# Sums of squares split before and after the product's end, and root and reciprocal on a 128x2 column of tokens, for the norms behind w_o and w_down

## The reference, cut to what matters

```python
def rms_norm(x, g):
    xf = x.astype(jnp.float32)
    y = xf * lax.rsqrt(jnp.mean(xf * xf, axis=-1, keepdims=True) + NORM_EPS)
    return (y * g.astype(jnp.float32)).astype(x.dtype)
...
        m = jnp.concatenate([a, p], axis=-1) @ w_o[l]
        x = x + rms_norm(m, post_mix_g[l])
        h = rms_norm(x, pre_ffn_g[l])
        up = causal_dwconv(h @ w_up[l], conv_w[l], conv_b[l])
        y = (jax.nn.gelu(up[..., :D_FF], approximate=True) * up[..., D_FF:]) @ w_down[l]
        x = x + rms_norm(y, post_ffn_g[l])
    return x
```

## Time and profile before

| | |
|---|---|
| time, median of 3 runs | 2281.69 us (2281.61 to 2284.61) |
| profiled execution: its time | 2283.57 us |
| profiled execution: its span on the core | 2281.8 us |
| PE busy | 2164.8 us (95%), 15448 instructions |
| DVE busy | 1486.6 us (65%) |
| ACT busy | 1077.4 us (47%) |
| POOL busy | 83.1 us (4%) |

### The profile page before, as it was taken

How to read it: one execution, slowest core, us unless ns; L and a number is a source line. 1 busy time by engine, 2 the same in 40 slices (tenths; PEclk the granted TensorE clock), 3 DMA queues, 4 the chain that set the end, 5 groups by cost and what they waited for, 6 DMA issues and landing times.

```text
span 2281.8 us, 39887 instructions
## 1 busy us (share of the span) xinstructions
PE 2164.8 (95%) x15448; PEld 1854.4 (81%) x15448; DVE 1486.6 (65%) x2015; ACT 1077.4 (47%) x1502; POOL 83.1 (4%) x70
## 2 busy tenths in 40 slices
PE   7999989999999999999899999987798999999996
PEld 6888868888888888887687878877686888888885
DVE  6656558885588856875974588853475544566654
ACT  5444555444444434445544655433343543556533
POOL 0800000000000000000000000002110000000000
PEclk9999989999999999999899999999999999999998
DMA  8654545665566556655355455643353555644551
GB/s 274 205 162 156 166 130 180 188 188 189 185 191 185 188 189 187 191 165 185 130 202 167 157 161 165 210 122 74 99 176 125 175 184 193 185 142 145 167 192 57
DMA packets 402679, 384.04 MB, mean 168 GB/s; under 512 B 43441, under 2 KB 401073, under 8 KB 401713
## 3 DMA queue, kind: packets, MB, share of 16 engines
q1 hardware_dynamic: 402546, 382.18, 53.9%
HBM read 374.78 MB, written 7.34 MB: 167 GB/s over the span
## 4 chain that ended last, share of the span: by engine, by line
PE 86%; DVE 8%; issue 2%; ACT 2%; DMA 1%; SPq 0%; DVEq 0%; POOL 0%; ACTq 0%
PE acc L746 44%; PE acc L749 22%; PE acc L770 3%; PE aux L1035 2%; PE acc L825 2%; PE acc L826 2%; PE acc L827 2%; PE acc L773 2%; DVE w_lo L1862 2%; PE acc L1035 1%; PE aux L843 1%; ACT w_hi L1274 1%; PE aux L1196 1%; PE aux L950 1%; PE aux L970 1%
## 5 line engine op out<-in xcount | busy, mean ns | idle before, releaser
L1862 DVE TENSOR_TENSOR w_lo<-raw_w,w_hi 128x1024 fp32r<-128x1024 f32 (+1 forms) x592 | 714.9, 1228 | 471.6 <-ACT w_hi L1274 470.5
L1274 ACT ACTIVATE w_hi<-raw_w 128x1024 fp32r<-128x1024 f32 (+1 forms) x592 | 613.0, 1046 | 686.3 <-PE acc L749 575.0
L746 PE MATMUL acc<-h,w_hi 128*128 128x512 f32 x1664 | 525.9, 397 | 1.2 <-DVE w_lo L1862 1.2
L749 PEld LDWEIGHTS acc<-h,w_lo 128*128 128x128 f32 x1664 | 312.6, 188 | 73.8
L749 PE MATMUL acc<-h,w_lo 128*128 128x256 f32 x1664 | 327.1, 278 | 0.0
L746 PEld LDWEIGHTS acc<-h,w_hi 128*128 128x128 f32 x1664 | 254.5, 189 | 2.2 <-issue 1.4
L746 PE MATMUL acc<-x_split,w_hi 128*128 128x512 f32 x704 | 225.2, 401 | 0.0
L746 PE MATMUL acc<-ff,w_hi 128*128 128x512 f32 x704 | 221.6, 396 | 2.4 <-DVE ff L2107 2.4
L746 PE MATMUL acc<-xs_b,w_hi 128*128 128x512 f32 x512 | 162.5, 399 | 1.7 <-DVE w_lo L2300 0.9
L749 PEld LDWEIGHTS acc<-ff,w_lo 128*128 128x128 f32 x704 | 132.2, 188 | 31.3
L749 PEld LDWEIGHTS acc<-x_split,w_lo 128*128 128x128 f32 x704 | 132.2, 188 | 31.2
(11 more groups left out here) (333 smaller groups left out, 3124.9 us busy)
## 6 DMA issues: line engine op xcount, KB each, us to landing
raw_w<-in_w_up SPq DMA_DIRECT2D x176, 512.0 KB, 3.5
raw_w<-in_a_w_in SPq DMA_DIRECT2D x128, 512.0 KB, 3.7
raw_w<-in_w_in SPq DMA_DIRECT2D x64, 512.0 KB, 4.0
raw_w<-in_w_down SPq DMA_DIRECT2D x64, 512.0 KB, 3.5
raw_w<-in_b_w_qg SPq DMA_DIRECT2D x64, 512.0 KB, 3.8
raw_w<-in_w_o SPq DMA_DIRECT2D x32, 512.0 KB, 3.5
raw_w<-in_a_w_out SPq DMA_DIRECT2D x32, 512.0 KB, 3.6
raw_w<-in_w_k_shared SPq DMA_DIRECT2D x32, 512.0 KB, 3.6
```

What stands on the lines that cost most here:

```text
L746: pe.matmul(ACC[2 * b + f], WHI[:, q, k, f * P:(f + 1) * P], op[:, kt, :, :].rearrange("p h t -> p (h t)"), start=first, stop=False)
L749: mm = pe.matmul(ACC[2 * b + f][:, 0:T], WLO[:, slot, k, f * P:(f + 1) * P], op[:, kt, 0, :], start=False, stop=last)
L1274: act.activation(WHI[:, u % 4, 0:ku, :], RAWW[:, u, 0:ku, :], ACT.Copy).then_inc(hi_made, 1)
L1862: dve.tensor_tensor(WLO[:, u, 0:ku, :], RAWW[:, u, 0:ku, :], WHI[:, u % 4, 0:ku, :].bitcast(F32), ALU.subtract)\
```

## The change

PE: the product and its sums become one function, `scaled_norm_gemm`. The sums of tiles 8 to 11 follow unit 27 instead of unit 31, and the last four tiles are no longer summed by `four_sums`. After the product `token_sums` takes the strips of the first twelve tiles (copied and scaled by DVE, with epsilon in them) and tiles 12 and 13, and then tiles 14 and 15, each as the stationary operand, against one column of ones: the sums come out as a column of tokens, 128x2, in PSUM. `spread_column` turns the 128x2 column of reciprocals into 128x256 by two matmuls with the identity.

ACT: in front of the last evacuation it takes the root of two ones (a dummy). After the last `by_gain` it takes the root of the 128x2 sums, scaled by 1/D, and only then splits unit 3. DVE: `first_groups` copies the strips in front of the last splits; after the last evacuation it takes the reciprocal of the 128x2 root, splits unit 3, and waits for the spread. `add_pair` reads the spread reciprocal from PSUM (AUX[2]) instead of N2[3].

```diff
+            ROOT2, RSTD2, AHEAD2 = (N2[1][:, 0, 0, 2 * k:2 * k + 2] for k in range(3))
...
+            def token_sums(bank, xs, start, stop):
+
+                for j, x in enumerate(xs):
+                    for t_ in range(2):
+                        mm = pe.matmul(bank[:, t_:t_ + 1], x[:, t_ * P:(t_ + 1) * P], ONES[:, 0:1],
+                                       start=(start and j + t_ == 0), stop=(stop and j == len(xs) - 1 and t_ == 1))
+                return mm
+
+            def spread_column(out, column, new=1):
+
+                pe.wait_ge(part_out, seen(part_out, new))
+                for t_ in range(2):
+                    mm = pe.matmul(out[:, t_ * P:(t_ + 1) * P], column[:, t_:t_ + 1].broadcast_to([P, P]), IDENT, start=True, stop=True)
+                mm.then_inc(y_sum, 1)
+
+            def scaled_norm_gemm(op, first=None, gates=[], ku=KU):
+
+                if first is not None:
+                    first()
+                for n in range(0 if first is None else 8, 32):
+                    if n < len(gates):
+                        pe.wait_ge(*gates[n])
+                    pe.wait_ge(lo_made, seen(lo_made))
+                    unit(op, n // 4 % 2, n % 4, n % 8, ku)
+                    if n in (15, 23, 27):
+                        pe.wait_ge(sq_ready, seen(sq_ready, 2))
+                        four_sums(AUX[0], SQY, (15, 23, 27).index(n), n == 15, n == 27)
+                pe.wait_ge(part_out, seen(part_out))
+                pe.wait_ge(sq_ready, seen(sq_ready))
+                token_sums(AUX[1], [N2[2], SQY[:, 12, :], SQY[:, 13, :]], True, False)
+                pe.wait_ge(sq_ready, seen(sq_ready))
+                token_sums(AUX[1], [SQY[:, 14, :], SQY[:, 15, :]], False, True).then_inc(y_sum, 1)
+                spread_column(AUX[2][:, 0:T], RSTD2)
...
-            gemm(4, B1, [], side=sum_of(SQY, AUX[0], ready=sq_ready),
-                 first=lambda: first_body(B1, [(pool_mix_ready, 8)] * 4 + [(mix_ready, 2 * n + 2) for n in range(4)], depth=DEPTH_W_O,
-                                          after={n: (lambda n=n: beside_unit(32 + n)) for n in range(8)}))
-            gather(AUX[0], N2[2])
+            scaled_norm_gemm(B1, lambda: first_body(B1, [(pool_mix_ready, 8)] * 4 + [(mix_ready, 2 * n + 2) for n in range(4)], depth=DEPTH_W_O,
+                                                    after={n: (lambda n=n: beside_unit(32 + n)) for n in range(8)}))
...
-                last = {"side": sum_of(SQY, AUX[0], ready=sq_ready)} if n == len(GROUPS) - 1 else {}
-                gemm(4, B2, quarters(gated_ready, tiles // 4), ku=tiles // 4, **last)
-            gather(AUX[0], N2[2])
+                if n < len(GROUPS) - 1:
+                    gemm(4, B2, quarters(gated_ready, tiles // 4), ku=tiles // 4)
+            scaled_norm_gemm(B2, gates=quarters(gated_ready, tiles // 4), ku=tiles // 4)
...
+            def root_of_sums(sums):
+                act.wait_ge(y_sum, sums)
+                act.activation(ROOT2, AUX[1][:, 0:2], ACT.Sqrt, scale=1.0 / D).then_inc(rstd_ready, 1)
+
+            def last_pair_and_root(sums):
+                for q in range(3):
+                    split_unit(q)
+                act.activation(AHEAD2, ONES[:, 0:2], ACT.Sqrt)
+                pend()
+                root_of_sums(sums)
+                split_unit(3)
+
             pend = gemm(4, copy_and_square(), keep=True, by_depth=True, written_out=True)
-            split(0, between=pend)
+            last_pair_and_root(2)
...
-            rsqrt(N2[2], N2[3])
...
-                link(dve.tensor_tensor(y2, y2, N2[3][:, :].unsqueeze(1).broadcast_to([P, 2, T]), ALU.mult))
+                link(dve.tensor_tensor(y2, y2, AUX[2][:, 0:T].unsqueeze(1).broadcast_to([P, 2, T]), ALU.mult))
...
+            def first_groups():
+                dve.wait_ge(y_part, seen(y_part))
+                dve.tensor_scalar(N2[2][:, :], AUX[0][:, 0:T], 1.0 / 32, NORM_EPS * D / P, ALU.mult, ALU.add).then_inc(part_out, 1)
+                seen(part_out)
+
+            def last_pair_and_reciprocal():
+                for q in range(3):
+                    split_unit(q)
+                pend()
+                dve.wait_ge(rstd_ready, seen(rstd_ready))
+                dve.reciprocal(RSTD2, ROOT2).then_inc(part_out, 1)
+                seen(part_out)
+                split_unit(3)
+                dve.wait_ge(y_sum, seen(y_sum, 2))
+
             pend = gemm(4, joiner(Y), keep=True, by_depth=True)
-            split(0, between=pend)
-
-
-            partial(AUX[0], N2[2])
-            variance(N2[2], beside_gemm=True)
-            dve.wait_ge(rstd_ready, seen(rstd_ready))
+            first_groups()
+            last_pair_and_reciprocal()
```

More of the change, by code:

```diff
@@ L1524, in _ @@
                 pend = gemm(4, (copier(), adder(), squarer())[n], pending=pend, ku=tiles // 4, keep=True, written_out=(n == 2))
-            split(0, between=pend)
-            rsqrt(N2[2], N2[3])
+            last_pair_and_root(5)
             def with_side(evac, side, per):
```

## The result

The changed kernel took 2267.07 us (median of 4 executions, 2266.45 to 2273.09), the kernel before beside it 2282.58 (4, 2281.61 to 2284.61): ratio 0.9937, 95% interval 0.9918 to 0.9955. Forecast were 2274.8, with a range of 2272.0 to 2278.8. The direction is right; the gain came out more than twice as large as forecast. Later series settle it lower: over 20 executions of the changed kernel (these four and sixteen more) the mean is 2271.8 (+-0.8, one standard error; 2266 to 2282), over 116 of the kernel before 2282.0 (+-0.2; 2274 to 2288). The gain is 10.2 us +-0.9, and a single kernel's executions scatter over 13 to 15 us. What is left to explain is about 3 us that the sum of 6.85 did not have.

The account below looks back on a forecast made before the run. PE bounds the kernel (86% of the span), standing still in serial hand-overs after w_o and w_down; 3.09 plus 3.76, together 6.85 us, off the median 2281.69 gave 2274.8, range 2272.0 to 2278.8.

Parts of the forecast that it names:

- the sum of 6.85: Forecast gain in us: 3.09 behind w_o (3.76 less 0.67 for moved sums) plus 3.76 behind w_down.
- the hand-over: Serial steps from a product's end to the first scaling behind w_o and w_down; at w_o 9.58 us before.
- the new order in it: After the last squares: token sums 1.15, root 0.22, then split branch 2.21 us; first scaling 3.76 earlier at both products.
- the later branch: Behind the root, unit 3's split (w_hi, w_lo) takes 2.21 us and outlasts the spread's 0.9 to 1.8.
- the spread: PE's two matmuls widening the reciprocal, bounded by 0.6 and 1.5 us; its branch stays under the split, costing nothing.
- The moved sums: Sums of tiles 8 to 11 behind unit 27: cost 0.67 us at w_o, covered after w_down.
- The dummy: ACT's early root pulls in the table load, 1.28 plus 0.17 us, inside idle time; free, 0.2 left at w_o.
- The first group of token matmuls: Twelve PE instructions from the product's end, 1.44 us, done before the squares at 2.24; at lower clock 0.6 late.
- the 1.03: Time in us from w_down's product end to DVE's evacuation; covers the moved sums' 0.67, leaving 0.36.
- the clock rivals: PE's clock after w_o: late rise pays back 1.5 us (2276.4, chance 0.10); kept clock gains up to 2.7 (2272.1, 0.10).
- Clock kept: Rival: the shorter gap behind w_o keeps PE's clock up, up to 2.7 us more gained, 2272.1; chance 0.10.
- Does the gain arrive?: Claim that PE carries w_o's gain on, and after w_down DVE starts its chain 3.76 us earlier.

Follow-up runs that it names:

- e7: Changed kernel with two useless DVE reciprocals of 128x256 before w_down's first scaling, a pure delay; ratio 0.998 to the kernel before.
- e9: Kernel before with two useless DVE reciprocals of 128x256 behind the root of w_down's norm; ratio 1.0026.
- e11: Changed kernel with one useless DVE reciprocal of 128x256 before w_down's first scaling; ratio 0.9966 to the kernel before.
- e5: Changed kernel without the dummy root ahead of the last evacuation; ratio 0.9975 to the kernel before.
- e4: Changed kernel with unit 3's w_hi made on ACT ahead of the last gain multiplication instead of behind the root; ratio 0.9954 to the kernel before.
- e6: Changed kernel with unread matmuls of ones filling PE's gaps behind w_o and w_down; 2265.87 us, ratio 0.9932 to the kernel before.
- f14: Kernel before with 26 unread matmuls of 128 columns in PE's gap behind w_o; ratio 0.9959.
- g15: Kernel before with 205 already met waits (103 instructions) at the head of PE's program; ratio 0.9978.
- g17: Changed kernel with 111 already met waits at the head of PE's program; ratio 0.9925 to the kernel before.
- e8: Kernel before with 47 already met waits at the head of PE's program, which became 24 instructions; ratio 1.0006.
- e2: Changed kernel with w_down as before, so only the norm behind w_o is changed; ratio 0.9987 to the kernel before.
- e3: Changed kernel with w_o as before, so only the norm behind w_down is changed; ratio 0.9974 to the kernel before.
- g16: Kernel before with 13 unread matmuls of 256 columns in PE's gap behind w_o, in place of f14's 26 of 128; ratio 0.9985.

## Why the prediction was right and where it was wrong

**Right, by the rows.** What bounds the hand-over, and the new order in it. From the start of the last sums to the scaling 3.58 were forecast (1.15 + 0.22 + 2.21); measured are 3.39 at both places, 1.09 up to ACT's root and 2.30 from there. From w_o's end to the scaling it is 5.54, forecast 5.82 (2.24 + 3.58). The split is the later branch and the spread 0.65 ahead of it, though the spread itself runs at the lower clock and takes 1.23, inside its bounds of 0.6 and 1.5. The moved sums cost 0.67 (1.36 less 0.69) by their round and 0.76 by the product's end. The dummy does not make the evacuation late: 0.04 behind PE. The gap of 0.02 behind the load (315.41 + 1.28, next at 316.71) again shows no drain; the Trainium skill, page "ScalarE: Activation LUTs", section "What ACT_TABLE_LOAD costs", which the prediction names, has one of some 1.38 us, and the trace does not agree with it. The first group of token matmuls, twelve instructions, runs at full clock beside the evacuation. After w_down the moved sums are covered, as the forecast had it: 0.26 of the 1.03 is left. Together 7.3 for 6.85. The terms that were off are small: 0.19 too much in these last steps at both places and 0.09 in the steps ahead of them, and at w_o the moved sums cost 0.09 more than their 0.67.

**Right, by experiment.** That PE carries the gain to the end: e7 and e9 give back at least what they delay (e11 1.5 of 1.8, within its error). That the load of the table must not stand behind the sums: e5. That the split sets the end: e4 takes it away and the spread is next at once.

**Undecided in the prediction, now seen.** Of the clock rivals neither came as put. The fall stays at 320.6. The rise follows the restart and comes 0.8 sooner after it than before; what that gives is up to 0.4 us (3.3 to 3.6 gained by 345 us for 3.28 at the scaling). "Clock kept" was priced at 2.7; e6 shortens the spell and has 2.1 to 2.4 of it. f14 loses no clock at all at w_o and gains 3.0, of which 0.5 is there at the restart already, since its gather takes 0.70 where before's takes 1.22.

**Wrong: "Does the gain arrive?", which took for granted that nothing but the two hand-overs moves.** This is the step that failed. I followed the gain down to the next waits of PE and stopped there, and so put everything behind at nothing. Of the 10.2 us the hand-overs are 7.5 (7.3 at the scalings, 0.2 from the clock), against 6.85; the rest, 2.7 us +-0.9, is what the sum lacked. The change adds 47 instructions to PE's program, and the rest goes with the second block's scan, 450 us further on, as the table has it: g15 and g17 show that the number of instructions alone moves the time by 6 to 7 us, and e8 and e2, whose scans are 2 to 3 us longer than before's, gain nothing by it (+1.3 and +0.5, within their errors of zero or nearly so). The row for this was on the page: "issue" has 2% of the chain, some 45 us, and no sentence of the prediction asked what it is.

**Wrong: the width.** The range rested on three executions spread over 3 us. The scatter is 13 us in before and 15 in the changed kernel, and the median of the changed kernel's first four lay 4.7 under its own mean. That the first comparison showed more than twice the forecast is this chance for the larger part (5.3 of the 8.7 that it has over 6.85). Even with the rest known, 2271.8 is outside the range at its lower end, by 0.2.

**Still open.** The traces make the scan 4 to 8 us shorter in the changed kernel, the means only 3; a part is lost between, or the profiled executions are not the mean; g15 has the same, 10 us in the trace and 6.4 in the mean. The rest of 2.7 is itself only three of its errors, and without the first four executions, which raised the question, it is 1.8 (sixteen executions, 2272.7 +-0.8). The direct control, before with exactly 47 instructions more, was not run: e8 had 24. That the changed kernel's own rest comes from the place of its boundaries is argued from the scans of its count (112 to 115 us in the seven traces with 47, 119 to 120 in the three with 0) and from g15 and g17 at other counts. e5 has the same count as the changed kernel and a rest of only -0.1. And e3 with 19 more has a shorter scan where e8 with 24 has a longer one: the count tells that the boundaries moved, but I did not work out beforehand which counts are good. Counted but not explained is also why a fetch is sometimes started late, up to 5.2 us after the boundary.

## What to carry to other kernels

A serial hand-over between two products can be priced from rows to within 0.5 us of 7; a column of tokens (128x2) for root and reciprocal, and sums moved ahead of the product's end, pay off as long as the table load goes ahead too. But in a long unrolled program each added instruction moves every later stage against the 256-instruction blocks, and a stage of many small matmuls answers with several us in either direction. Before a gain of under 0.5% is put down to an edit, measure it at several lengths of the program: satisfied waits at the head, where TensorE stands idle for 15 us anyway, deal the boundaries anew. The fastest kernels here are two at 2264 to 2265: the changed one with filled gaps and w_hi ahead (f13), and the changed one with nothing but 111 idle waits (g17).

## What the runs showed of the hardware

- PE stalls at instruction numbers that are multiples of 256, until 1.1 to 1.6 us after a 16 KB packet of the instruction queue has landed; 321 of 321 gaps over 0.5 us in the scan that have no wait of their own, up to 5.0 us long.
- Two waits on a semaphore in a row became one instruction: 47 gave 24, 205 gave 103.
- Matmuls with one moving column (128x128 fp32 weights) take 0.13 us an instruction, eight in 1.05. In the changed kernel PE runs twenty of them in the gap behind w_o, and the granted clock falls at 320.6 as in before, which has none. With unread matmuls of 128 columns in f14's gap it did not fall there at all, and with such of 256 columns in e6's the low spell was 3.4 us instead of 10.2.
- The same filling does not always work: f14 restarts behind w_o at 2.4 GHz, g16, with the gap filled for the same time, had its fall 1 us before the restart (327.95, restart 328.96) and gained 0.3 instead of 3.0.
